# First pair's q and k normed from unscaled sums in PSUM, with x's sums of squares by pairs of tiles and the second chunk of weights rounded in halves

## What is computed

```python
h = rmsnorm(x, g_mix)
q_sb, k_sb, v_sb, q_r, k_r, v_r, g_r, gate_sb, gate_ret = split_cols(h @ w_in)
q_sb = head_rmsnorm(to_heads(q_sb, SB_HEADS), sb_q_gain)     # per head of 64: x * rsqrt(mean(x*x) + EPS) * gain
k_sb = head_rmsnorm(to_heads(k_sb, SB_HEADS), sb_k_gain)
y_sb = from_heads(stick_breaking_attention(q_sb, k_sb, to_heads(v_sb, SB_HEADS)))
q_r, k_r = rotary(...), rotary(...) * (RET_QK_DIM ** -0.5)
y_r = from_heads(head_rmsnorm(retention_chunkwise(q_r, k_r, v_r), ret_norm_gain)) * silu(g_r)
merged = sigmoid(gate_sb) * (y_sb @ w_branch_sb) + sigmoid(gate_ret) * (y_r @ w_branch_ret)
x = x + merged @ w_out
```

## Time and profile before

| | us |
|---|---|
| median of 3 runs (902.05 to 902.13) | 902.12 |
| the profiled execution | 901.76 |
| its span | 900.0 |
| TensorE busy | 892.2 (99%) |
| VectorE busy | 516.4 (57%) |
| ScalarE busy | 400.3 (44%) |
| GpSimd busy | 18.0 (2%) |

### The profile page before, as it was taken

One profiled execution on the slowest core, in us unless ns is written; L12 is line 12 of the kernel. 1 busy time (PEld: TensorE's weight loads), 2 busy tenths in 40 slices (PEclk: granted clock), 3 DMA queues, 4 the chain that ended last, 5 costly groups with the idle time before them and its releaser, 6 DMA issues.

```text
span 900.0 us, 11499 instructions
## 1 busy us (share of the span) xinstructions
PE 892.2 (99%) x4098; PEld 727.3 (81%) x4098; DVE 516.4 (57%) x657; ACT 400.3 (44%) x521; POOL 18.0 (2%) x19
## 2 busy tenths in 40 slices
PE   9999999999999999999999999999999999999998
PEld 6777887887887888888888888888888888888886
DVE  7797677677677443333455666556666543333454
ACT  6656746746746632232345333333333332323431
POOL 1410000000000000000000000000000000000000
PEclk9999999999999999999999999999999999999999
DMA  8114114115114153223322322222222332322241
GB/s 288 71 43 168 48 40 172 47 38 171 48 35 153 54 205 103 86 89 105 117 94 95 115 94 93 101 102 101 93 93 93 91 101 88 106 87 93 65 146 64
DMA packets 28698, 89.95 MB, mean 100 GB/s; under 512 B 3936, under 2 KB 5232, under 8 KB 28544
## 3 DMA queue, kind: packets, MB, share of 16 engines
q1 hardware_dynamic: 27376, 85.87, 27.8%
q10 hardware_dynamic: 1072, 3.67, 1.3%
q0 software_dynamic: 224, 0.06, 0.1%
HBM read 84.34 MB, written 2.10 MB: 96 GB/s over the span
## 4 chain that ended last, share of the span: by engine, by line
PE 93%; DVE 4%; ACT 1%; DMA 1%; issue 1%; SPq 0%; DVEq 0%
PE dense L387 29%; PE dense L389 28%; PE dense L388 28%; PE z L444 2%; DVE lo L1146 1%; DVE fs L1143 1%; PE aty L475 1%; DVE w_lo L1143 1%; PE aty L389 1%; PE aty L388 1%; DVE fs L1327 1%; PE aty L387 1%; DMA fs<-in_xT 1%; PE aty L433 1%; PE aty L494 0%
## 5 line engine op out<-in xcount | busy, mean ns | idle before, releaser
L387 PE MATMUL dense<-hi,w_hi 128*128 128x512 f32 x1166 | 461.1, 395 | 0.5 <-DVE lo L1146 0.3
L389 PE MATMUL dense<-hi,w_lo 128*128 128x512 f32 x1166 | 454.4, 390 | 0.0
L388 PE MATMUL dense<-lo,w_hi 128*128 128x512 f32 x1166 | 454.2, 390 | 0.0
L1143 DVE TENSOR_TENSOR w_lo<-w_f,w_hi 128x1024 fp32r<-128x1024 f32 (+2 forms) x160 | 185.5, 1159 | 228.0 <-ACT w_hi L708 227.2
L387 PEld LDWEIGHTS dense<-hi,w_hi 128*128 128x128 f32 x1166 | 218.9, 188 | 50.4 <-issue 4.4
L389 PEld LDWEIGHTS dense<-hi,w_lo 128*128 128x128 f32 x1166 | 218.8, 188 | 46.1
L388 PEld LDWEIGHTS dense<-lo,w_hi 128*128 128x128 f32 x1166 | 219.1, 188 | 42.9 <-issue 0.5
L708 ACT CAST w_hi<-w_f 128x1024 fp32r<-128x1024 f32 (+2 forms) x160 | 158.3, 990 | 174.7 <-PE dense L389 172.1
L1143 DVE TENSOR_TENSOR fs<-fs 128x512 f32<-128x512 f32 (+3 forms) x120 | 87.9, 738 | 3.8 <-ACT fs L740 0.5
L693 ACT ACTIVATE fs<-fs 128x512 f32<-128x512 f32 (+2 forms) x79 | 55.1, 703 | 50.7 <-DVE fs L1146 38.6
L1143 DVE TENSOR_TENSOR lo<-fs,hi 128x512 fp32r<-128x512 f32 (+3 forms) x67 | 50.5, 761 | 41.4 <-ACT hi L1076 20.2
(11 more groups left out here) (103 smaller groups left out, 438.8 us busy)
## 6 DMA issues: line engine op xcount, KB each, us to landing
w_f<-in_w_in SPq DMA_DIRECT2D x52, 512.0 KB, 3.3
w_f<-in_w_up SPq DMA_DIRECT2D x44, 512.0 KB, 3.2
w_f<-in_w_down SPq DMA_DIRECT2D x16, 512.0 KB, 3.4
w_f<-in_w_b SPq DMA_DIRECT2D x8, 512.0 KB, 3.2
w_f<-in_w_out SPq DMA_DIRECT2D x8, 512.0 KB, 3.2
w_f<-in_w_pg SPq DMA_DIRECT2D x8, 512.0 KB, 3.2
w_f<-in_w_down SPq DMA_DIRECT2D x8, 384.0 KB, 3.0
fs<-in_xT SPq DMA_DIRECT2D x4, 512.0 KB, 7.0
```

The lines of the kernel that those rows point to most:

```text
L387: mm(out, w1, x1, start=start, stop=False, skip_group_check=skip)
L388: mm(out, w1, x0, start=False, stop=False, skip_group_check=skip)
L389: return mm(out, w0, x1, start=False, stop=stop, skip_group_check=skip)
L1143: return nc.vector.tensor_tensor(out, a, b, op).then_inc(done, 1)
```

## The change

- x's squares: `raw_square` takes two tiles in one instruction, and `raw_sum` adds them as pairs into two rows, and those two at the end. The first double square stands behind tile 5.
- Chunk 1's weights are rounded and subtracted in halves of four tiles; its first matmul waits for the first half (s_w1lo), the fifth tile for the second.
- q and k of pair 0 are no longer scaled. `first_square_of` squares the bank, `first_stat` adds by head into `z`, and `first_variance` adds EPS times x's variance (with its own EPS as eps_sq): for u = h / r, mean(h h) + EPS = r r (mean(u u) + EPS / (r r)), and 1 / (r r) is mean(x x) + EPS. `first_log`, `first_exp` take the factor, and `first_norm` multiplies the bank by it.
- The banks: chunks 3 and 4 go to banks 0 and 1 (they wait for s_nrm), not to `aty`.
- The order of pair 0: hooks of slots 3 to 8 move ahead, the second head's `sb_values` from slot 8 to slot 7; the orders of ScalarE and VectorE change with them; the decay load moves behind chunk 6's.

```diff
-            load_fac(0)
             for c in range(3, 8):
                 load(c, c % RING, w_in[c], 8)
+                if c == 6:
+                    sp.wait_ge(s_stat, 2)
+                    load_fac(0)
...
+            def first_stat(t):
+                pe.wait_ge(s_cst, 16)
+                pe.wait_ge(s_fsq, t + 1)
+                mm(z[:, t, :], cst[:, C_BLOCK, :], first_square(t), start=True, stop=True).then_inc(s_stat, 1)
...
-                    places = {(3, 1): at(stat_qk, 0, 1, (s_misc, 1)), (3, 7): at(sb_scores, j, 0),
-                              (4, 1): at(turn_v, 0, 2, (s_misc, 2)), (5, 0): at(sb_scores, j, 1),
-                              (5, 2): at(sb_turn, j, 0), (5, 7): at(sb_values, j, 0, 3), (6, 1): at(sb_scores, j, 2),
-                              (6, 3): at(sb_turn, j, 1), (7, 0): at(sb_values, j, 0, 2), (7, 3): at(sb_turn, j, 2),
-                              (7, 6): at(sb_values, j, 0, 1), (7, 7): at(sb_values, j, 0, 0)}
+                    places = {(3, 2): at(sb_scores, j, 0), (3, 5): at(turn_v, 0, 2, (s_misc, 2)),
+                              (4, 0): at(sb_scores, j, 1), (4, 1): at(sb_turn, j, 0), (4, 7): at(sb_values, j, 0, 3),
+                              (5, 3): at(sb_scores, j, 2), (5, 4): at(sb_turn, j, 1), (6, 0): at(sb_values, j, 0, 2),
+                              (6, 3): at(sb_turn, j, 2), (6, 6): at(sb_values, j, 0, 1), (6, 7): at(sb_values, j, 0, 0)}
+                    first = 7
...
                 for n in range(NT):
-                    places[8, 1 + n] = at(sb_values, j, 1, NT - 1 - n)
+                    places[first, 1 + n] = at(sb_values, j, 1, NT - 1 - n)
...
-                    if prev is not None or s in (5, 8):
+                    if prev is not None or s > 4:
                         free_bank(j, s)
+                    else:
+                        pe.wait_ge(s_nrm, s - 2)
...
-            chunk(1, 1, 1, KD, T_X0)
-            chunk(2, 2, 2, KD, T_X0, {0: stat_x, 6: lambda: stat_qk(0, 0, (s_xrs, 1))})
+            chunk(1, 1, 1, KD, T_X0, {3: lambda: first_stat(0)}, before={4: (s_wlo, 2)}, halved=True)
+            chunk(2, 2, 2, KD, T_X0, {0: stat_x, 1: lambda: first_stat(1)})
```

ScalarE:

```diff
-                if k in (3, 5):
-                    raw_square(k // 2 - 1)
-            high(0, 1, first=True)
-            for k in range(2, KD):
-                raw_square(k)
+                if k == 5:
+                    raw_square(0)
+            act.wait_ge(s_wdma[1], 16)
+            nc.scalar.copy(w_hi[1][:, 0:4, :], w_f[1][:, 0:4, :]).then_inc(s_w1hi, 1)
+            nc.scalar.copy(w_hi[1][:, 4:8, :], w_f[1][:, 4:8, :]).then_inc(s_whi, 1)
+            raw_square(1)
+            first_square_of(0)
+            raw_square(2)
+            high(0, 2, first=True)
+            raw_square(3)
...
             def start():
-                high(0, 2, first=True)
                 ahead(0, 1)
+                first_square_of(1)
+                ahead(0, 2)
                 act.wait_ge(s_xst, 1)
+                run(fs[:, A_G + 1, :], misc, ACT.Identity, s_xvar, scale=EPS * 64 / D)
                 run(fs[:, A_RS, :], misc, ACT.Ln, s_xln, scale=1.0 / D, bias=eps[:, :])
+                first_log(0)
                 act.wait_ge(s_xln, 1)
                 run(fs[:, A_RS, :], fs[:, A_RS, :], ACT.Exp, s_xrs, scale=-0.5)
-                ahead(0, 2)
-                norm_qk(0, 0, 1)
+                first_log(1)
+                first_exp(0)
+                first_exp(1)
                 high_qk(0, 0)
-                norm_qk(0, 1, 2)
                 high_qk(0, 1)
                 sigmoid_tables()
-                ahead(0, 3)
...
                 sb_factors(0, 0)
+                ahead(0, 3)
                 high_v(0, 0)
                 high_h(0)
                 high_h(1)
                 ahead(0, 4)
-                high_h(2)
                 sb_high(0, 0)
                 sb_factors(0, 1)
+                high_h(2)
                 high_h(4)
...
                 y_out(0, 0)
                 ahead(0, 7)
                 high_h(7)
+                y_move(0, 0)
+                y_out(0, 1)
                 silu(0)
                 high_rot(0, 1)
-                y_move(0, 0)
-                y_out(0, 1)
```

VectorE:

```diff
             def start():
+                first_variance(0)
+                first_variance(1)
+                dve.wait_ge(s_cr, 7)
+                ahead(0, 2)
+                first_norm(0)
+                first_norm(1)
+                low_qk(0, 0)
+                low_qk(0, 1)
                 dve.wait_ge(s_xrs, 1)
-                dve.wait_ge(s_cr, 7)
-                evac_x(0)
-                square(0, 0)
-                evac_x(1)
-                square(0, 1)
-                ahead(0, 2)
-                norm(0, 0)
-                low_qk(0, 0)
-                norm(0, 1)
-                low_qk(0, 1)
                 evac_x(2)
-                ahead(0, 3)
                 dve.wait_ge(s_rope, 16)
...
                 sb_weights(0, 0)
                 low_v(0, 0)
+                ahead(0, 3)
                 low_h(0)
                 low_h(1)
                 evac_x(3)
+                sb_low(0, 0)
                 ahead(0, 4)
+                sb_weights(0, 1)
+                low_h(2)
                 evac_x(4)
-                low_h(2)
-                sb_low(0, 0)
-                sb_weights(0, 1)
                 low_h(4)
                 ahead(0, 5)
+                sb_low(0, 1)
                 evac_x(5)
+                sb_weights(0, 2)
                 low_h(3)
-                sb_low(0, 1)
-                sb_weights(0, 2)
+                ahead(0, 6)
+                sb_low(0, 2)
+                evac_x(6)
                 low_h(5)
-                ahead(0, 6)
-                evac_x(6)
-                low_h(6)
-                sb_low(0, 2)
                 turned(0, 0)
                 low_rot(0, 0)
+                low_h(6)
                 ahead(0, 7)
                 low_h(7)
```

More of the change, by code:

```diff
@@ L108, in build @@
         eps = sb("eps", [P, 1], F32)
+        eps_sq = sb("eps_sq", [P, 1], F32)
         bank = [ctx.enter_context(nc.psum_tensor(f"dense{b}", [P, SEQ], F32)) for b in range(3)]
@@ L389, in split3, with chunk @@
                 return mm(out, w0, x1, start=False, stop=stop, skip_group_check=skip)
-            def chunk(c, r, b, kt, tile0, hooks=None, k_first=0, last=True, before=None, out=None):
-                pe.wait_ge(s_wlo, c + 1)
-                out = bank[b][:, :] if out is None else out
+            def chunk(c, r, b, kt, tile0, hooks=None, k_first=0, last=True, before=None, halved=False):
+                if halved:
+                    pe.wait_ge(s_w1lo, 1)
+                else:
+                    pe.wait_ge(s_wlo, c + 1)
+                out = bank[b][:, :]
                 for k in range(kt):
@@ L573, in back @@
                               for k in range(KD)} if prev is None and s == RAW_X else None
-                    out = aty[:, s - 2, :] if prev is None and s in (3, 4) else None
-                    chunk(SLOTS * j + s, s % RING, s % 3, KD, T_X0 if raw else T_H, hooks, before=before, out=out)
+                    chunk(SLOTS * j + s, s % RING, s % 3, KD, T_X0 if raw else T_H, hooks, before=before)
             def stat_x():
                 pe.wait_ge(s_cst, 16)
-                pe.wait_ge(s_xacc, KD)
+                pe.wait_ge(s_xacc, 4)
                 stat(C_ONES, A_G, s_xst)
@@ L708, in high, with raw_square, first_square_of @@
                 nc.scalar.copy(w_hi[r][:, 0:kt, :], w_f[r][:, 0:kt, :]).then_inc(s_whi, 1)
-            def raw_square(k):
-                if k >= 4:
-                    act.wait_ge(s_xacc, k - 3)
-                run(fs[:, A_T + k % 4, :], fs[:, A_X + k, :], ACT.Square, s_xsq)
+            def raw_square(p):
+                if p >= 2:
+                    act.wait_ge(s_xacc, p - 1)
+                rows = A_T + 2 * (p % 2)
+                run(fs[:, rows:rows + 2, :], fs[:, A_X + 2 * p:A_X + 2 * p + 2, :], ACT.Square, s_xsq)
+            def first_square_of(t):
+                act.wait_ge(s_used, t + 1)
+                run(first_square(t), bank[t][:, :], ACT.Square, s_fsq)
             act.wait_ge(s_gmix, 16)
@@ L749, in square_high, with first_log, first_exp @@
                 run(hi[:, T_SQ, :], fs[:, a_raw(j, t), :], ACT.Square, s_sqhi)
+            def first_log(t):
+                act.wait_ge(s_fvar, t + 1)
+                sq = fs[:, a_sq(0, t), :]
+                run(sq, sq, ACT.Ln, s_misc, scale=1.0 / 64, bias=eps_sq[:, :])
+            def first_exp(t):
+                sq = fs[:, a_sq(0, t), :]
+                act.wait_ge(s_misc, t + 1)
+                run(sq, sq, ACT.Exp, s_rs, scale=-0.5)
             def norm_qk(j, t, free):
@@ L1154, in _ @@
             nc.vector.memset(eps[:, :], EPS).then_inc(s_eps, 1)
+            nc.vector.memset(eps_sq[:, :], EPS * EPS).then_inc(s_eps, 1)
             nc.vector.memset(hi[:, T_SQ, :].bitcast(F32), 0.0).then_inc(s_warm, 1)
```

(2 more changed lines are left out.)

79 lines of the change are left out of this document (43 added, 36 removed).

## The result

The changed kernel takes 908.26 us (median of 4 runs, 907.76 to 908.80) against 902.12 before: ratio 1.0068, interval 1.0054 to 1.0081, that is 6.1 us slower. The prediction said slower, 906.0, with 903.3 to 908.0 as its range: the side was right, the size too small, and the time lies 0.3 us above the range. The four runs form two pairs, 907.8 and 907.9 with a mean granted clock of 0.998, and 908.7 and 908.8 with 0.995 and 0.996. The profiled run is one of the latter: 908.67, span 906.9. Two of the four runs so lie inside the predicted range, and the median outside it.

What follows compares the result with a forecast made beforehand. TensorE, busy 892.2 of 900.0 us, was taken as the bound, so only its first-pair stalls counted: 1.15 + 3.2 + 3.6 = 7.95 after against 3.9 before, taken as +3.9 on 902.12, giving 906.0 us, range 903.3 to 908.0.

Steps and rivals of the forecast that it cites:

- part 4: Second head's values in chunk 7: TensorE waits 3.6 us for y_out(0,0), queued behind high_rot(0,0) and VectorE's rotation.
- Part 3: Hooks in chunks 4 to 6: VectorE, slowed by GpSimd, stalls TensorE 2.0 us at (4,7), 3.2 together with smaller waits.
- the walk: VectorE's and GpSimd's queues followed in turns of whole instructions, GpSimd's at 1.25 us each, giving the 2.0 us stall.
- The lead of q and k: Pair 0's q and k: scans begin at 33.85 instead of 37.61, so the attention chain starts 3.75 us sooner.
- Part 1: Start, chunks 0 and 1: tile 6 later, chunk 1 without a wait; stalls 1.35 us before, 1.15 after.
- The sum without the clock: First pair's TensorE stalls, 7.95 us after against 3.9 before: taken as +3.9 us, with nothing for a clock fall.
- parts 1 to 3: The start, q and k, and the hooks in chunks 4 to 6: stalls after of 1.15 and 3.2 us.
- The rival's price: Clock falls in the 3.6 us stall: +1.8 us, from the first 22 matmuls' 6.8 against 5.0, giving 907.8; chance 12%.

Runs made afterwards that it cites:

- experiment 1: Changed kernel with y_out(0, 0) ahead of high_rot(0, 0) in ScalarE's queue: 902.29 us, ratio 1.0006.
- experiment 2: Changed kernel with 14 unread matmuls of 512 columns filling TensorE's stall before the second head's first values product, the wait kept: 905.81 us, ratio 1.0045.
- experiment 6: Changed kernel with GpSimd's wait for the rounded q and k taken off, so its eight products start earlier: 905.75 us, ratio 1.0042.
- experiment 8: Changed kernel with y_out(0, 0) ahead of high_rot(0, 0) on ScalarE and the attention's own steps first on VectorE: 899.05 us, ratio 0.9969.
- experiment 9: Kernel of experiment 8 with the first double square of x given back as two single ones, behind tiles 3 and 5: 898.62 us, ratio 0.9964.
- experiment 5: Changed kernel with sb_low(0, 0) ahead of low_h(0), low_h(1) and evac_x(3) in VectorE's queue: 906.41 us, ratio 1.0054.
- experiment 4's first kernel: Kernel before with one more table load (1.28 us) on ScalarE ahead of y_out(0, 0): 904.21 us, ratio 1.0023.
- experiment 3: Changed kernel with the second head's values products back in slot 8: 904.72 us, ratio 1.0035.
- experiment 4's kernels with two and four loads: Kernel before with two table loads of different sets, or with four loads, ahead of y_out(0, 0): 906.26 us and 909.33 us.

## Why the prediction was right and where it was wrong

- **The stall of part 4 (3.6 us): right.** `y_out` started 4.6 us after VectorE's `evac_x(6)` (65.80 against 61.24) and TensorE went on at 66.43, which is 5.4 behind chunk 6's end at about 61.04, as worked out. Measured as a wait 3.4, as a difference of experiments 1 and 2 3.5.
- **Part 3 (the hooks in chunks 4 to 6): right in kind and nearly in size.** A stall of 2.0 was predicted at (4,7), the trace has 2.0 (43.81 + 0.23 to 46.04), from a queue that was walked by turns with GpSimd. The four small ones behind it, put at 0.2, 0.4, 0.4 and 0.2, are 0.3, 0.3, 0.4 and 0.2 by TensorE's starts. Experiment 6 shows that GpSimd is the cause: moved in time, the stretching moves with it. That the two take turns by whole instructions, as the walk had it, fits the durations and was not tested by itself. The Trainium skill (GPSIMD Engine Reference, 1. Specifications) names this contention for VectorE instructions with two SBUF inputs; the trace agrees, since the scans over PSUM keep 2.33 us beside GpSimd (the same at 118.04, with GpSimd idle) while h 0 and h 1 go from 1.40 to 3.48.
- **The lead of q and k: right.** The scans begin at 34.41 instead of 37.61 (33.85 predicted): a lead of 3.2 us where 3.75 was predicted, 0.3 of the difference being the late transfer of the next point. That lead only pays once the orders let it: it is what experiment 8 cashes in.
- **Part 1 (the start, 0.2 us won): right in the whole change, by cover.** In experiment 1's profile, whose start is the changed kernel's, ScalarE begins tile 4 at 9.80 as before, and chunk 1 starts at 15.06 (15.08 predicted). In the changed kernel's own profile it starts at 15.38, because this transfer landed 0.3 us later:

```profile
10.14 1.34 ACT L704 ACTIVATE hi<-fs,gain 128x512 fp32r<-128x512 f32 x2 [0.40 <-DMA fs<-in_xT]
```

```profile
9.80 1.34 ACT L704 ACTIVATE hi<-fs,gain 128x512 fp32r<-128x512 f32 x2 [0.39 <-DMA fs<-in_xT]
```

The first row is the changed kernel's, the second experiment 1's. Alone, this part costs 0.95, because x's statistic then comes late; the prediction saw that the sums end 0.2 us ahead of their need in the whole change, and that held only by the head statistic in front of it. The double square's delay of tile 6 is in the prediction (12.0 instead of 11.57); experiment 9 shows that giving the square back, with the halves kept, wins 0.4.
- **The sum without the clock** was +0.45 for parts 1 to 3 and +3.6 for part 4. Measured: +0.5 (experiment 1, not told from nothing) and +3.5. TensorE's idle time grew by 3.7, where the forecast added 3.9.
- **The step that failed is the clock.** The sum put it at nothing. It stood among the rivals, at 12% and +1.8 us, where it belonged into the sum: the predicted stall brought it in all four runs, at 2.15 us on the median. The 12% came from nothing but that no stall of before had done it, the longest being 0.7 us. With experiments 1 and 2 the account closes: 3.9 + 2.15 = 6.05 against the measured 6.1.
- **The rival's price** came from 22 matmuls at the start. That they ran at the lower level was read from their pace alone: up to 0.43 us a matmul, as behind the stall. The granted clock of those microseconds is 1.00 in the table by single microseconds too, so it isn't the page's coarseness that hides it, and no granted clock shows the 1.8. In the changed kernel's profile the same matmuls take 7.8 us instead of 6.8. That the rival's 907.8 meets the two faster runs is in part luck.
- The Trainium skill (TensorE: Matmul & The Clock Gate, HAM oscillation) says that waits between bursts can bring the engine back to half clock. By that rule the sum would have been 906.0 and the 1.8 us of the earlier trace rows, 907.8, or with the 2.15 of experiment 2 908.15, and the trace agrees, with the clock at 0.50 from 66 to 72 us.
- **A label:** the 0.52 us of the single square (11.05 to 11.57) is read from the earlier trace rows, not the earlier trace rows.

## What to carry to other kernels

When a dependent step moves ahead in TensorE's order, look in the other engines' queues for what stands in front of the instruction that releases it, not only for when its data are there: here a copy that was ready waited over 4 us behind a cast that was not. Price a new stall of TensorE twice, once as itself and once for the clock behind it: here stalls of 3.3 us and more always brought the half clock (20 runs of 20), those of 2.0 us in half of the runs, and the 0.7 of the kernel before did not. If the stall can't be avoided, filling it with matmuls whose result nobody reads gets most of the second part back. One instruction over two tiles saves an issue (0.96 us instead of two of 0.52 here), but what waits behind it waits for both tiles: here the next urgent tile, at 0.4 us.

## What the runs showed of the hardware that had not been expected

A stall of 2.0 us was followed by the half clock in eleven of twenty runs of one and the same program, at 1.1 us; 3.3 us in all four, at 1.8 on the median; 5.9 us in all four, at 2.3. Whether a given run loses depends on something that the program doesn't set, and two groups of times a microsecond apart are its mark.

The groups go with how long the clock stays low. In the profiles of experiment 5 (mean clock 0.998), of experiment 4's first kernel (0.997) and of experiment 3 (0.998) it was low for 3.4 us, in those of the changed kernel (0.995), of experiment 6 (0.995) and of experiment 4's kernels with two and four loads (0.996) for 6.8 us. Behind the stall the shorter stretch cost 1.6 us by the rows (5.0 us for instructions that take 3.4 to 3.5 at full clock), the longer one 2.6 to 2.9. That fits the changed kernel's two groups, 907.8 at a clock of 0.998 and 908.7 at 0.995 and 0.996: 1.8 and 2.7 us for the clock. Its 907.8 runs have no profile, so for them this is inferred. The fall itself didn't always come while TensorE stood still: in experiment 5 it came half a microsecond after TensorE had resumed, in experiment 3 1.4 us after.
